# Chunked recurrence on one core: 128x128 transposes for the transposed products, and four array tiles for the turned keys, the remainder and the inverse

## The reference

```
def step(state, inp):                       # state: 64x64 for each head
    r_t, w_t, k_t, v_t, kk_t, a_t = inp
    sa = einsum('bhij,bhj->bhi', state, -kk_t)
    state = state * w_t + sa[..., None] * (kk_t * a_t)[:, :, None, :] + v_t[..., None] * k_t[:, :, None, :]
    return state, einsum('bhij,bhj->bhi', state, r_t)
y = scan(forward) + scan(reverse)
```

## Time and profile before

| | |
|---|---|
| median of 3 runs | 3892.47 us (3888.59 to 3895.09) |
| profiled execution: its span, and the only time known of it | 3891.5 us |
| PE busy in the span | 3726.6 us (96%) |
| DVE, ACT, POOL busy | 1682.0, 1439.6, 1385.9 us |
| mean granted clock of TensorE | 0.991 |
| recurrence of the first layer, about | 138 to 372 us |
| recurrence of the second layer, about | 1258 to 1492 us |

### The profile page before, as it was taken

How to read it: one execution, slowest core, us unless ns; L and a number is a source line. 1 busy time by engine, 2 the same in 40 slices (tenths; PEclk the granted TensorE clock), 3 DMA queues, 4 the chain that set the end, 5 groups by cost and what they waited for, 6 DMA issues and landing times.

```text
span 3891.5 us, 67184 instructions
## 1 busy us (share of the span) xinstructions
PE 3726.6 (96%) x28976; PEld 2991.8 (77%) x28976; DVE 1682.0 (43%) x2714; ACT 1439.6 (37%) x2450; POOL 1385.9 (36%) x581
## 2 busy tenths in 40 slices
PE   8888999999999889999999999999999999999999
PEld 7777768888887776688888876578888776688887
DVE  6554441477245554612683158515111376332112
ACT  3454252323323442523223243634222436433222
POOL 5001324444443002144444454234444453244443
PEclk9999999999999999999999999999999999999999
DMA  3001212266221001122473222112322221122222
GB/s 146 2 4 46 84 67 96 87 248 235 87 87 44 4 4 66 70 112 87 162 269 142 87 98 76 44 68 100 108 87 90 105 87 65 45 87 87 87 108 87
DMA packets 37151, 356.66 MB, mean 92 GB/s; under 512 B 4224, under 2 KB 4352, under 8 KB 17920
## 3 DMA queue, kind: packets, MB, share of 16 engines
q1 hardware_dynamic: 19584, 278.93, 19.4%
q10 hardware_dynamic: 17280, 73.48, 5.3%
HBM read 350.29 MB, written 2.10 MB: 91 GB/s over the span
## 4 chain that ended last, share of the span: by engine, by line
PE 84%; DVE 7%; ACT 4%; issue 2%; DMA 1%; PEld 1%; POOL 0%; PEldq 0%; DVEq 0%; SPq 0%; ACTq 0%; POOLq 0%
PE banks L768 23%; PE banks L770 23%; PE banks L769 23%; PE banks L1127 10%; PE banks L2179 3%; ACT arena L2335 2%; ACT arena L1495 2%; PE banks L2261 1%; DMA ring<-stream 1%; DVE arena L1975 1%; DVE arena L1869 1%; PE banks L1249 0%; DVE x L2736 0%; PE banks L1447 0%; DVE arena L1986 0%
## 5 line engine op out<-in xcount | busy, mean ns | idle before, releaser
L866 POOL TENSOR_TENSOR ring_r<-ring,hi_ring 128x1024 fp32r<-128x1024 f32 x490 | 1204.4, 2463 | 2176.6 <-ACT hi_ring L857 2176.2
L768 PE MATMUL banks<-xT_r,ring_r 128*128 128x512 f32 (+1 forms) x2480 | 951.9, 384 | 11.9 <-issue 7.9
L770 PE MATMUL banks<-xT_r,hi_ring 128*128 128x512 f32 x2096 | 826.5, 394 | 0.0
L769 PE MATMUL banks<-x_lo_r,hi_ring 128*128 128x512 f32 x2096 | 823.3, 393 | 0.0
L857 ACT ACTIVATE hi_ring<-ring 128x1024 fp32r<-128x1024 f32 x490 | 511.2, 1047 | 719.6 <-DMA ring<-stream 302.3
L768 PEld LDWEIGHTS banks<-xT_r,ring_r 128*128 128x128 f32 x2480 | 470.3, 190 | 108.5 <-issue 15.8
L770 PEld LDWEIGHTS banks<-xT_r,hi_ring 128*128 128x128 f32 x2096 | 394.2, 188 | 92.6
L769 PEld LDWEIGHTS banks<-x_lo_r,hi_ring 128*128 128x128 f32 x2096 | 396.4, 189 | 89.2 <-issue 3.3
L1127 PE MATMUL banks<-arena 64*64 64x64 f32 (+4 forms) x7456 | 341.9, 249 | 53.4 <-DVE arena L1869 22.8
L1495 ACT ACTIVATE arena<-banks 128x512 f32<-128x512 f32 x366 | 214.6, 595 | 402.0 <-PE banks L770 242.9
L770 PE MATMUL banks<-hi_ring,pairs 128*128 128x512 f32 x864 | 342.5, 396 | 0.0
(11 more groups left out here) (262 smaller groups left out, 5393.0 us busy)
## 6 DMA issues: line engine op xcount, KB each, us to landing
ring<-stream SPq DMA_DIRECT2D x132, 2048.0 KB, 7.7
arena<-ada ACTq DMA_DIRECT2D x96, 512.0 KB, 5.1
arena<-ln_rows ACTq DMA_DIRECT2D x5, 1024.0 KB, 7.8
arena<-edge ACTq DMA_DIRECT2D x4, 1024.0 KB, 5.0
arena<-edge ACTq DMA_DIRECT2D x2, 1792.0 KB, 7.6
arena<-pack ACTq DMA_DIRECT2D x2, 1485.0 KB, 6.9
arena<-pack ACTq DMA_DIRECT2D x2, 1200.5 KB, 5.5
x<-x_in SPq DMA_DIRECT2D x4, 512.0 KB, 7.5
```

The source lines that it names most:

```text
L768: first = nc.tensor.matmul(out_, left[1], right[0], start=start, stop=False)
L769: low = nc.tensor.matmul(out_, left[0], right[1], start=False, stop=False)
L770: return first, low, nc.tensor.matmul(out_, left[0], right[0], start=False, stop=stop)
L866: nc.gpsimd.tensor_tensor(feed.raw(n, ring_r), feed.raw(n), feed.hi(n).bitcast(F32), ALU.subtract).then_inc(split_lo, 1)
```

## The change

The transposed products `inv_t` of levels 0 to 3 go. In their place `inv_r` n transposes the new X with four transposes of 128x128; it stands in the next beat, behind `inv_a` n+1, and is copied by ACT. `inv_t` 4 stays. `turned` 0 and `r0` go; one step `ar` makes both results, 32 products in four tiles into two banks, in the beat where `turned` 2 was, which moves to the beat of `turned` 0. `wu` crosses for half of its products and so uses four tiles; its halves by bank are now those of the row half, so both banks are full only at its end. In all steps with four tiles each row half now has a bank of its own. Level 0 of `inv_a` moves to bank 6.

```diff
@@ -164,13 +164,12 @@
     b0, b1 = ((0, 1), (2, 3))[d]
     turned = [("v_rows", j, (6,))] if d == 0 else []
     out = [[("prep", g, (b0, b1))], [], [("prep_w", g, ())], [], [("prep_a", g, ())], [], [("prep_b", g, ()), ("prep_ar", g, ())],
-           [("gram", g, 0, (b0, b1))], [("gram", g, 1, (b0, b1)), ("unit", g, ())], [("turned", g, 0, (6,))] + turned,
-           [("x0", g, (b0,)), ("turned", g, 1, (b1,))], [("turned", g, 2, (6,))]]
+           [("gram", g, 0, (b0, b1))], [("gram", g, 1, (b0, b1)), ("unit", g, ())], [("turned", g, 2, (6,))] + turned,
+           [("x0", g, (b0,)), ("turned", g, 1, (b1,))], [("ar", g, (b0, b1))]]
     for n in range(len(LEVELS)):
         last = n == len(LEVELS) - 1
-        banks_a, banks_x, banks_t = (b0,), (b0,) if n else (6,), (b0,) if n == 0 or last else (6,)
-        out += [[("inv_a", g, n, banks_a)] + ([("r0", g, (6,))] if last else []),
-                ([] if last else [("inv_x", g, n, banks_x)]) + [("inv_t", g, n, banks_t)]]
+        out += [[("inv_a", g, n, (b0,) if n else (6,))] + ([("inv_r", g, n - 1, (6,))] if n else []),
+                [("inv_t", g, n, (b0,)) if last else ("inv_x", g, n, (b0,) if n else (6,))]]
     out += [[("wu", g, (b0, b1))], [("mq", g, (b0, b1))], [("oo", g, ())]]
     out += [[("link", g, i, (4 + i % 2,) if i < NC - 1 else ())] for i in range(NC)]
...
-    AR0 = [arena[:, a_:a_ + 1024].rearrange("p (q e a t) -> p q e a t", q=4, e=2, a=2) for a_ in (22888, W_HI)]
+    AR0 = [arena[:, a_:a_ + 1024].rearrange("p (q b t) -> p q b t", q=4, b=4) for a_ in (22888, W_HI)]
...
-        return name == "inv_t" and level in (0, len(LEVELS) - 1) or name in ("inv_a", "inv_x") and level > 0
+        return name in ("inv_a", "inv_x", "inv_t") and level > 0
...
@@ -1245,56 +1244,78 @@
                 b = banks[0]
                 take(b, use[0])
                 for q in range(4):
-                    src = ARI[g % 3][:, 0, q * P:(q + 1) * P] if which == 0 else BB[g % 2][:, which - 1, q * P:(q + 1) * P]
-                    ins = nc.tensor.transpose(bank[b][:, q * P:(q + 1) * P], src, C("ident"))
+                    ins = nc.tensor.transpose(bank[b][:, q * P:(q + 1) * P], BB[g % 2][:, which - 1, q * P:(q + 1) * P], C("ident"))
                 ins.then_inc(bank_full[b], 1)
-            elif name in ("x0", "r0", "inv_a", "inv_x", "inv_t"):
+            elif name == "ar":
+                g, d = args[0], args[0] % 2
+                for b, m in zip(banks, use):
+                    take(b, m)
+                drained(pe, uses, "gram", g, 1)
+                drained(pe, uses, "v_rows", g // 2)
+                for a in range(2):
+                    for q in range(4):
+                        for k, r in HALVES:
+                            p_, e = (r ^ k, r) if a == 0 else (r, r ^ k)
+                            left, right = (GM[d][side(p_), q, e, 1, 0, :], V[g // 2 % 2][side(p_), q, e, :]) if a else \
+                                (ARI[g % 3][side(e), 0, (2 * q + p_) * CH:(2 * q + p_ + 1) * CH], C("ident2")[side(e)])
+                            ins = mm(bank[banks[r]][side(k), (4 * a + q) * CH:(4 * a + q + 1) * CH], left, right, True, True)
+                            if (a, q, k) == (1, 3, 1):
+                                ins.then_inc(bank_full[banks[r]], 1)
+            elif name in ("x0", "inv_a", "inv_x", "inv_t"):
 
                 g, d = args[0], args[0] % 2
                 for b, m in zip(banks, use):
                     take(b, m)
                 if name == "x0":
                     pe.wait_ge(first_done, g + 1)
-                elif name == "r0":
-                    drained(pe, uses, "gram", g, 1)
-                    drained(pe, uses, "v_rows", g // 2)
                 elif name != "inv_a":
                     drained(pe, uses, "inv_a", g, args[1])
                     if args[1]:
-                        drained(pe, uses, "inv_t", g, args[1] - 1)
+                        drained(pe, uses, "inv_r", g, args[1] - 1)
                 elif args[1]:
                     drained(pe, uses, "inv_x", g, args[1] - 1)
                 else:
                     drained(pe, uses, "x0", g)
                 level = args[1] if len(args) > 1 else 0
                 for q in range(4):
-                    for e in range(2):
-                        for p_ in range(2):
-                            n, straight, crossed = 2 * q + e, side(p_), side(p_ ^ e)
-                            h = crossed if level and name in ("inv_x", "inv_t") else straight
-                            to = crossed if name == "inv_a" and level or name == "inv_t" and level < len(LEVELS) - 1 else straight
-                            left, right = {"x0": (XT[d][h, n, :], C("ident2")[h]), "r0": (GM[d][h, q, e, 1, 0, :], V[g // 2 % 2][h, q, e, :]),
-                                           "inv_a": (GM[d][h, q, e, 0, 0, :], X[d][h, n, :]), "inv_x": (XT[d][h, n, :], T1[d][h, n, :]),
-                                           "inv_t": (T1[d][h, n, :], XT[d][h, n, :])}[name]
-                            at = (4 * e + q if wide(name, level) else n) * CH
-                            to = across(banks[0])[to, at:at + CH] if wide(name, level) else bank[banks[0]][to, at:at + CH]
-                            ins = mm(to, left, right, True, True)
+                    for k, p_ in HALVES if wide(name, level) else ():
+                        if name == "inv_a":
+                            e = p_ ^ k
+                            left, right, to, at = GM[d][side(p_), q, e, 0, 0, :], X[d][side(p_), 2 * q + e, :], side(e), 4 * p_ + q
+                        else:
+                            p_, e = p_ ^ k, p_
+                            turned_, t1 = XT[d][side(e), 2 * q + p_, :], T1[d][side(e), 2 * q + p_, :]
+                            left, right = (turned_, t1) if name == "inv_x" else (t1, turned_)
+                            to, at = side(p_ if name == "inv_x" else p_ ^ e), 4 * e + q
+                        ins = mm(across(banks[0])[to, at * CH:(at + 1) * CH], left, right, True, True)
+                    for e, p_ in () if wide(name, level) else HALVES:
+                        h, n = side(p_), 2 * q + e
+                        left, right = {"x0": (XT[d][h, n, :], C("ident2")[h]), "inv_a": (GM[d][h, q, e, 0, 0, :], X[d][h, n, :]),
+                                       "inv_x": (XT[d][h, n, :], T1[d][h, n, :])}[name]
+                        ins = mm(bank[banks[0]][h, n * CH:(n + 1) * CH], left, right, True, True)
+                ins.then_inc(bank_full[banks[0]], 1)
+            elif name == "inv_r":
+
+                g, level = args
+                take(banks[0], use[0])
+                drained(pe, uses, "inv_x", g, level)
+                for q in range(4):
+                    ins = nc.tensor.transpose(bank[banks[0]][:, q * P:(q + 1) * P],
+                                              X[g % 2][:, 2 * q:2 * q + 2, :].rearrange("p e t -> p (e t)"), C("ident"))
                 ins.then_inc(bank_full[banks[0]], 1)
             elif name == "wu":
                 g, d = args[0], args[0] % 2
                 for b, m in zip(banks, use):
                     take(b, m)
-                drained(pe, uses, "turned", g, 0)
-                drained(pe, uses, "r0", g)
+                drained(pe, uses, "ar", g)
                 drained(pe, uses, "inv_t", g, len(LEVELS) - 1)
                 for q in range(4):
-                    for e in range(2):
-                        for p_ in range(2):
-                            h = side(p_)
-                            ins = mm(bank[banks[q // 2]][h, (q % 2 * 2 + e) * P:(q % 2 * 2 + e + 1) * P], XT[d][h, 2 * q + e, :],
-                                     AR0[d][h, q, e, :, :].rearrange("p a t -> p (a t)"), True, True)
-                    if q % 2:
-                        ins.then_inc(bank_full[banks[q // 2]], 1)
+                    for e, r in HALVES:
+                        p_ = r ^ e
+                        ins = mm(bank[banks[r]][side(p_), q * P:(q + 1) * P], XT[d][side(r), 2 * q + e, :],
+                                 AR0[d][side(r), q, e:p_ + 3:2 + p_ - e, :], True, True)
+                        if (q, e) == (3, 1):
+                            ins.then_inc(bank_full[banks[r]], 1)
...
@@ -1563,25 +1584,25 @@
                 g, which = args
                 d = g % 2
                 filled(b, n)
-                out_ = AR0[d][:, :, :, 0, :] if which == 0 else GM[d][:, :, :, which - 1, 2, :]
-                f(out_, bank[b][:, :].rearrange("p (q e k) -> p q e k", q=4, e=2), ACT.Copy).then_inc(bank_free[b], 1)
+                f(GM[d][:, :, :, which - 1, 2, :], bank[b][:, :].rearrange("p (q e k) -> p q e k", q=4, e=2), ACT.Copy).then_inc(bank_free[b], 1)
             elif name in ("inv_x", "inv_t") and wide(name, args[1]):
                 filled(b, n)
                 f((XT if name == "inv_t" else X)[args[0] % 2].rearrange("p (q e) t -> p e q t", e=2),
```

(25 more changed lines are left out.)

4 lines of the change are left out of this document (2 added, 2 removed).

## The result

| | before | after |
|---|---|---|
| median of 4 runs each | 3892.64 us (3888.59 to 3895.09) | 3923.73 us (3915.37 to 3927.60) |
| ratio, 95% interval | | 1.0076 [1.0064, 1.0089] |
| span of the profiled execution | 3891.5 us | 3925.8 us |
| mean granted clock | 0.991 | 0.980 |

Slower by 31 us. Forecast was 3892, range 3868 to 3907: wrong, and outside the range.

What follows compares the result with a forecast made beforehand. PE was taken as the bound after `gram` 1, but copies on ACT and DVE within the inverse. Waits of 2.6 us a layer, +5 in two, with (a) -2.5 and (b) -3 gave -0.5: 3891.0 profiled, median 3892, range 3868 to 3907.

Steps and rivals of the forecast that it cites:

- odd groups: Period of an odd group, from `prep` to the next `prep`: 29.00 before to 29.09 us, +0.1 each.
- even groups with the first: Even groups: +0.1 us in the levels and +0.1 from `gram` on, +0.2 each; the first group's levels and `gram` part likewise.
- (a): Four-tile steps, each row half writing its own bank: 0 to 0.06 us saved a step, 0 to -5 us, taken as -2.5.
- (b): PE pauses inside steps that no semaphore explains, cheaper in steps gone or beside a wait: 0 to -10 us, taken as -3.
- a rival, to which I gave 0.07: Emptier inverse levels let PE's clock fall, 1.5 to 5.4 us each; in 14 inversions +42, 3934 us; chance 0.07.
- `inv_a` 2 to 3, the new wait: `prep_a` behind the copy of `inv_r` 1 on ACT delays X: odd groups 3.40 to 4.49 us, even 3.99 to 4.49.
- `gram` on DVE's chain: `inv_a` 3 to `gram` 0 stays 4.03 us, since DVE's operations hid `inv_t` 3; its removal gives nothing.
- `x0` in even groups: `x0` waits for `first_done` on DVE, going from 6.74 to 6.53 us; 0.65 of `wu`'s 0.86 turns into a wait.
- `wu` in an odd group: With `v_rows` ahead, `wu` is late enough that its saving of 0.86 us counts in full.
- transposes don't overlap: Four `inv_r` transposes take 1.15 us, not 0.66, +0.49 at each of four levels: +31, 3923 us; chance 0.03.
- ACT's order: `prep_a` behind `inv_r` 1 costs 0.5 to 1 us more in 14 inversions, `inv_a` 2 to 3 passing 5: 3903; chance 0.10.
- PE time (0.19): Copies and PE overlap better, so 1.9 us of PE work a group pays: -30, 3862 us, half 3877; chance 0.19.

Runs made afterwards that it cites:

- fill8: Changed kernel plus eight unread 64x64 products in two tiles behind `inv_x` 1 to 3, into bank 6; 3911.7 us.
- late: Changed kernel with `prep_a` one beat later, behind the copies of X on ACT; 3906.4 us.
- tiles: Changed kernel with the inverse of before (`inv_t` products kept, `inv_t` 4 in two tiles), new `ar` and `wu`; 3911.8 us.
- late_turn: Changed kernel with `prep_a` one beat later and three unread transposes of T1 behind `inv_x` 1 to 3; 3895.2 us.
- late_fill: Changed kernel with `prep_a` one beat later and eight unread two-tile products behind `inv_x` 1 to 3; 3903.8 us.

## Why the prediction was wrong

Profiled executions, 3891.5 to 3925.8, +34.3. The groups are sums of their undisturbed distances:

| part | predicted | measured |
|---|---|---|
| start of a layer, at full clock, x2 | +2.8 | +2.6 |
| odd groups, x6 | +0.6 | +1.4 (29.0 to 29.23) |
| even groups with the first, x8 | +1.8 | +5.5 (28.33 to 28.95; the first +0.9) |
| last group, x2 | 0 | -1.1 |
| (a) a bank for each row half | -2.5 | 0 |
| (b) pauses | -3 | -3.2 |
| clock, within the recurrences | 0 | +17.9, what is left of the recurrences' +23.2 |
| outside the recurrences | 0 | +11.1 |

- **The failed step: the sum has no term for the clock.** It was left to a rival, to which I gave 0.07, "Against it: the whole stretch has 0.99 ..., with like pauses". The pauses weren't like: PE waits for about 1.2 twice in a group now, ahead of `inv_a` 3 and of `gram`, where its longest wait by a semaphore in groups 1 to 6 was 0.74, and its busy time in the first layer's stage is 11 us less. (The mean of 0.99 in the earlier trace rows is 3% of that stretch at half clock, not the 1% that I had.) Within the two recurrences TensorE was at 1.2 GHz for 17 us before and for 73 after. That the emptier inverse would let the clock fall was told rightly; the price of 1.5 to 5.4 us a fall, in 14 inversions, was too dear: there were 7 falls in groups 1 to 6, 1.2 us for one of 3.4 us beside `gram` 0, and 2.9 for one of 13.7 at a layer's start. `fill8` shows the cause: -12 us for wasted work. The 17.9 is found by subtraction and isn't measured alone.
- **Outside the recurrences.** 5 of the 11 us stand right behind the two stages, where falls last 10.2 us in the one and 17.1 and 3.4 in the other, in place of 6.8 in each. The other 6 are in the second block, which the change doesn't touch, most of them at a fall of 10.2 at 2549 us that before doesn't have. Over the kernels what lies outside the recurrences is 3414 to 3426 us with no order in it that I could find. That is open.
- **`inv_a` 2 to 3, the new wait: right.** 4.55 in both kinds of group (4.49 forecast), by `prep_a` in ACT's order; `late` shows it, -0.95. `inv_a` 1 to `inv_x` 1 2.06 (1.98), `inv_x` 1 to `inv_a` 2 1.49 (1.44), `inv_a` 0 to 1 4.46, 0.40 less where I had 0.47.
- **`gram` on DVE's chain: right.** `inv_a` 3 to `gram` 0 is 3.98 where I had 4.03; and right that `r0`'s 0.9 buys nothing there. Wrong that `gram` 1 comes 0.1 sooner: still 2.59 behind `gram` 0.
- **`x0` in even groups: half right.** It waits for `first_done`, but didn't come sooner (6.7 behind `gram` 0 before and after, where I had 6.53), so `wu`'s 0.86 went wholly into the wait (`wu` to `mq` 3.42, now 3.43). That is 0.21 of the 0.42 by which the even groups lost more than forecast. `inv_a` 2 to 3 is another 0.17: undisturbed it was 3.88, and the 3.99 that I had read was a disturbed one. The copies are 0.15 (0.51 in place of 0.42 ahead of `inv_x` 1, 0.40 in place of 0.47 ahead of `inv_a` 1), and `ar` gives 0.12 back.
- **`wu` in an odd group:** `wu` to `mq` went from 3.42 to 2.54, -0.88: right. `ar` between `mq` and `oo` +0.24, in even groups +0.19 (+0.31 forecast).
- **(a) fell.** `inv_a` 1 has 15.4 ns a pass before and after. `mq`'s 13.4 for half its columns was no row for it (its passes follow at 27.6 ns, not 26.8). So the rule of the Trainium skill, TensorEngine Tiling (Array Packing), Gotcha 1: PSUM Pressure, that different row tiles can't use one bank at the same time, shows neither as a serialization nor as (a).
- **(b) was right in size, without its cause.** In `tiles` the same term is +8: pauses belong to how fast passes follow each other, not to the steps they stand in.
- **The other rivals.** That transposes don't overlap was wrong: within a block they start 128 ns apart in the mean (165, then 109 and 109). ACT's order stayed under its 5 us. PE time (0.19) was wrong too: `wu` paid in odd groups, where PE was the bound; else each saving met a copy, a mask or an instruction packet.

## What to carry to other kernels

Work taken off an engine between two waits may be worth nothing, and it can even cost: look at the granted clock in the emptiest stretch of the profile and ask what the change empties further; a cheap unread step in the gap tells whether the clock is the price. When a step's inputs change engine, the place of every other long operation in that engine's order has to be chosen anew, and a place that is good for one order is bad for the other. In stages of very short matmuls count instructions as well as time.

## What the runs showed of the hardware

- PE pauses inside steps of short passes. 137 pauses of 0.35 to 1.8 us, all ending 1.19 to 1.61 us behind the landing of a 16,384-byte instruction packet; up to 18.5 us in one execution (`tiles`). There is one such packet for some 130 fp32 passes.
- A block of four transposes between steps of tiles starts 0.15 us behind the start of the last pass ahead of it (that pass's recorded end is 0.07 later still), and inside it they follow at 128 ns in the mean, while each is recorded with 0.29 us.
- Three unread transposes behind `inv_x` 1 to 3 kept the clock at full speed in groups 1 to 6 (`late_turn`, no falls) where without them there were three falls (`late`), as eight unread products did (`late_fill`). The clock was 0.987 to 0.992, 0.983 to 0.989 and 0.987 to 0.991 in the runs of the three.
